# The second half of a closing RMS norm: factor from a square root and a reciprocal of two columns, sent over a diagonal

## What is computed

```python
def rmsnorm(x, g):
    y = x * lax.rsqrt(jnp.mean(x * x, axis=-1, keepdims=True) + 1e-6)
    return y * g

x = x + 0.5 * swiglu(rmsnorm(x, ffn2_norm), w_gate, w_up, w_down)
return rmsnorm(x, final_norm)
```

## Time and profile before

| | |
|---|---|
| median of 3 runs | 1667.12 us (1665.48 to 1675.3: 1675.3, 1667.12, 1665.48) |
| the profiled execution, its own time | 1676.78 us |
| span of the profiled execution | 1675.0 us |
| outside the span | 1.78 us |
| mean granted TensorE clock | 0.986 of full |

### The profile page before, as it was taken

One profiled execution on the slowest core, in us unless ns is written; L12 is line 12 of the kernel. 1 busy time (PEld: TensorE's weight loads), 2 busy tenths in 40 slices (PEclk: granted clock), 3 DMA queues, 4 the chain that ended last, 5 costly groups with the idle time before them and its releaser, 6 DMA issues.

```text
span 1675.0 us, 22081 instructions
## 1 busy us (share of the span) xinstructions
PE 1643.0 (98%) x8648; PEld 1327.8 (79%) x8648; DVE 813.1 (49%) x1342; ACT 686.1 (41%) x1232; POOL 267.2 (16%) x225
## 2 busy tenths in 40 slices
PE   9999999899999999999999999999999999999997
PEld 6777777777888888877888888877877888888887
DVE  5566435556655542255444433347465544443333
ACT  7565546545443343245333333344133533333222
POOL 1221110301322220002222210000020032223000
PEclk9997989999999999999999999999999999999999
DMA  5221000222333333313332233332222233222332
GB/s 197 77 89 39 15 26 14 95 81 88 101 101 101 101 92 94 97 58 113 101 101 92 97 92 103 87 119 83 70 87 83 95 101 101 92 97 86 104 97 79
DMA packets 45399, 148.50 MB, mean 89 GB/s; under 512 B 5193, under 2 KB 8433, under 8 KB 45297
## 3 DMA queue, kind: packets, MB, share of 16 engines
q1 hardware_dynamic: 41760, 142.10, 27.2%
q10 hardware_dynamic: 3536, 5.00, 0.9%
HBM read 144.98 MB, written 2.10 MB: 88 GB/s over the span
## 4 chain that ended last, share of the span: by engine, by line
PE 92%; DVE 3%; ACT 3%; issue 1%; DMA 1%; POOL 0%; DVEq 0%; SPq 0%; ACTq 0%; POOLq 0%
PE bank L257 90%; PE bank L378 1%; DMA raw<-in_w_in 1%; ACT hi L998 0%; DVE lo L1661 0%; PE bank L430 0%; ACT sq L1017 0%; PE bank L438 0%; DVE acc L1677 0%; DMA raw<-in_w_out 0%; ACT L1028 0%; DVE hs L2362 0%; DVE B L2284 0%; DVE x L2429 0%; DVE y L2219 0%
## 5 line engine op out<-in xcount | busy, mean ns | idle before, releaser
L1661 DVE TENSOR_TENSOR lo<-raw,hi 128x512 fp32r<-128x512 f32 (+1 forms) x514 | 392.2, 787 | 603.6 <-ACT hi L998 603.3
L257 PE MATMUL bank<-xh,hi 128*128 128x512 f32 x1576 | 613.2, 396 | 6.5 <-issue 2.0
L257 PE MATMUL bank<-xh,lo 128*128 128x512 f32 x1576 | 603.5, 390 | 1.2 <-DVE lo L1661 1.2
L257 PE MATMUL bank<-xl,hi 128*128 128x512 f32 x1576 | 596.3, 390 | 0.0
L998 ACT ACTIVATE hi<-raw 128x512 fp32r<-128x512 f32 (+1 forms) x540 | 321.6, 616 | 458.2 <-PE bank L257 413.9
L257 PEld LDWEIGHTS bank<-xh,hi 128*128 128x128 f32 x1576 | 296.2, 188 | 79.7 <-issue 10.9
L257 PEld LDWEIGHTS bank<-xh,lo 128*128 128x128 f32 x1576 | 296.6, 188 | 64.6 <-DVE lo L1661 2.1
L257 PEld LDWEIGHTS bank<-xl,hi 128*128 128x128 f32 x1576 | 296.6, 188 | 63.4 <-issue 3.1
L257 PE MATMUL bank<-fH,hi 128*128 128x512 f32 (+1 forms) x550 | 210.1, 382 | 0.0
L257 PE MATMUL bank<-fH,lo 128*128 128x512 f32 (+1 forms) x550 | 209.3, 381 | 0.0
L257 PE MATMUL bank<-fL,hi 128*128 128x512 f32 (+1 forms) x550 | 209.3, 381 | 0.0
(11 more groups left out here) (387 smaller groups left out, 1147.2 us busy)
## 6 DMA issues: line engine op xcount, KB each, us to landing
raw<-in_ffn_w_up SPq DMA_DIRECT2D x88, 512.0 KB, 3.4
raw<-in_w_in SPq DMA_DIRECT2D x50, 512.0 KB, 3.5
raw<-in_ffn_w_down SPq DMA_DIRECT2D x48, 512.0 KB, 3.5
raw<-in_ffn_w_gate SPq DMA_DIRECT2D x44, 512.0 KB, 3.5
raw<-in_ffn_w_down SPq DMA_DIRECT2D x24, 384.0 KB, 3.0
raw<-in_w_out SPq DMA_DIRECT2D x16, 512.0 KB, 3.4
x<-in_xt SPq DMA_DIRECT2D x8, 256.0 KB, 6.0
x<-in_xt ACTq DMA_DIRECT2D x8, 256.0 KB, 5.1
```

The lines of the kernel that those rows point to most:

```text
L257: return pe.matmul(out, w, x, start=start, stop=stop, skip_group_check=True)
L1661: dve.tensor_tensor(k.lo[i % CUT][:, 0:w], k.raw[u % RAW][:, at:at + w], k.hi[i % CUT][:, 0:w].bitcast(F), SUB).then_inc(k.cut_tail[i % 2], 1)
```

## The change

For the second half (h = 1) alone, the way from the squares to the factor is another one:

- TensorE, `row_sums`: now the blocks of `acc` and `sq[1]` are the weights and one column of ones the moving operand, two blocks of 128 tokens each. The result has tokens on partitions: 128x2. The `acc` part that stood after t = 12 is gone from the loop and stands after it, ahead of the wait for the square.
- ScalarE, `root`: square root of (sum/1024 + eps), 128x2, out of PSUM. `root_table` (a one-element Sqrt) takes the place of `log_table`.
- VectorE, `diagonal`: reciprocal of the 128x2, then the identity times it, a 128x256 tile in `acc2` with the factors on two diagonals.
- TensorE, `row_factor`: ones as weights by that tile, 256 columns: the factor of each token in every partition, in PSUM.
- VectorE, `write(1, n)`: reads the factor from PSUM instead of from `rB`.
- VectorE: `last_tile(1)` stands after all eight writes of the first half instead of after four, followed by `diagonal`.

A tile `rt` of 128x4 is allocated after `acc2`, so what is allocated behind it moves.

```diff
+COLS = [slice(0, 256), slice(256, 512)]
+HALVES = {7: -1}
@@ TensorE
+def row_sums(pe, k, i, h):
+    b, n = k.uses.take(("norm", i, h), 7)
+    room(pe, k, b, n)
+    pe.wait_ge(k.both, i + 1)
+    out, blocks = k.bank[b], [slice(256 * h + 128 * c, 256 * h + 128 * c + 128) for c in range(2)]
+    for c, at in enumerate(blocks):
+        mm(pe, out[:, c:c + 1], k.acc[:, at], k.ones[:, 0:1], c == 0, False)
+    pe.wait_ge(k.last_sq, k.last_sq_at[i] + h)
+    for c, at in enumerate(blocks):
+        m = mm(pe, out[:, c:c + 1], k.sq[1][:, at], k.ones[:, 0:1], False, True)
+    m.then_inc(k.full[b], 1)
+
+def row_factor(pe, k, i, h):
+    b, n = k.uses.take(("factor", i, h), 6 + h)
+    room(pe, k, b, n)
+    pe.wait_ge(k.diagonal, HALVES[i] + h + 1)
+    mm(pe, k.bank[b][:, COLS[h]], k.ones, k.acc2[:, COLS[h]], True, True).then_inc(k.full[b], 1)
@@ tensor_finale
-            if h == 1 and t == 12:
-                last_sums(pe, k, 1, cols[1])
-    end_last_sums(pe, k, 1, cols[1])
+    row_sums(pe, k, 7, 1)
+    row_factor(pe, k, 7, 1)
@@ ScalarE
+def root_table(act, k):
+    act.activation(k.eps[:, 2:3], k.eps[:, 0:1], ACT.Sqrt)
+
+def root(act, k, i, h):
+    b, _ = k.uses.at["norm", i, h]
+    act.wait_ge(*k.full_at(("norm", i, h)))
+    act.activation(k.rt[:, 2 * h:2 * h + 2], k.bank[b][:, 0:2], ACT.Sqrt, scale=1.0 / 1024,
+                   bias=k.eps[:, 0:1]).then_inc(k.read[b], 1)
@@ scalar_finale
     last_factor(0)
-    log_table(act, k)
+    root_table(act, k)
     last_square(1)
-    last_factor(1)
+    root(act, k, 7, 1)
@@ VectorE
+def diagonal(dve, k, i, h):
+    at, r = HALVES[i] + h + 1, k.rt[:, 2 * h:2 * h + 2]
+    dve.wait_ge(*k.read_at(("norm", i, h)))
+    dve.reciprocal(r, r).then_inc(k.inverted, 1)
+    dve.wait_ge(k.inverted, at)
+    dve.tensor_tensor(k.acc2[:, COLS[h]].rearrange("p (c t) -> p c t", c=2),
+                      k.ident.unsqueeze(1).broadcast_to([128, 2, 128]), r.unsqueeze(2).broadcast_to([128, 2, 128]),
+                      MUL).then_inc(k.diagonal, 1)
@@ vector_finale, write(h, n)
-        dve.wait_ge(k.rB_made, 8 + h)
+        if h == 0:
+            dve.wait_ge(k.rB_made, 8)
+        else:
+            dve.wait_ge(*k.full_at(("factor", 7, 1)))
+        factor = k.bank[k.uses.at["factor", 7, 1][0]] if h else k.rB
-        dve.scalar_tensor_tensor(..., scalar=k.col("final_norm_2", n), in1=k.rB[:, o],
+        dve.scalar_tensor_tensor(..., scalar=k.col("final_norm_2", n), in1=factor[:, o],
@@ vector_finale, loop over stores
-        if i == 4:
+        if i == 8:
             last_tile(1)
+            diagonal(dve, k, 7, 1)
@@ build
-        k.acc, k.acc2 = new("acc", T), new("acc2", T)
+        k.acc, k.acc2, k.rt = new("acc", T), new("acc2", T), new("rt", 4)
+        k.inverted, k.diagonal = sem("inverted"), sem("diagonal")
```

More of the change, by code:

```diff
@@ L2425, in write @@
         o = cols[h]
-        dve.wait_ge(k.rB_made, 8 + h)
+        if h == 0:
[3 more added lines that the diff above has]
+        factor = k.bank[k.uses.at["factor", 7, 1][0]] if h else k.rB
         if n == 7:
             dve.wait_ge(*k.read_at(("last", h)))
-        dve.scalar_tensor_tensor(out=k.xt[n][:, o], in0=k.xt[n][:, o], scalar=k.col("final_norm_2", n), in1=k.rB[:, o],
+        dve.scalar_tensor_tensor(out=k.xt[n][:, o], in0=k.xt[n][:, o], scalar=k.col("final_norm_2", n), in1=factor[:, o],
                                  op0=MUL, op1=MUL).then_inc(k.normed, 1)
```

## The result

The changed kernel's median is 1693.64 us (1693.28 to 1706.4, six runs) against 1666.97 us for the kernel before (1665.07 to 1678.79, six runs). The ratio, changed kernel to kernel before, is 1.0166, 95% interval 1.0135 to 1.0197. It is 27 us slower, where no measurable change was forecast, and far outside the range. The profiled execution took 1706.4 us, with a span of 1704.6 us against 1675.0; its mean granted clock was 0.984 against 0.986, so the two traces can be compared.

What follows compares the result with a forecast made beforehand. The prediction took the TensorE matmul stream (92% of the span) as the bound, with only the tail reachable: -0.72 us from square to first write and -0.04 from the add, -0.76 off 1667.12, giving 1666.4 us, range 1664.4 to 1674.6.

Steps and rivals of the forecast that it cites:

- The matmuls at either end alone: Whole kernel: a stream of matmuls, 92% TensorE; the change reaches only the last 9.37 us and some matmuls just before.
- Rival 3: All matmuls: tiles moved by rt change the pitch, 1% or 15 us slower, 1682; chance 0.03.
- The acc sum: End of the matmul stream: ends 0.43 us earlier, but the last add moves only -0.04, bounds -0.43 and +0.17.
- Narrow sums: Tail, TensorE after the square: four passes taking 0.52 us, ends 0.35 and 0.66, replacing 0.71.
- Root: Tail, ScalarE: 128x2 square root out of PSUM taking 0.25 us, ends 0.19 and 0.35; no table load on the path.
- Reciprocal and product: Tail, VectorE `diagonal`: the pair takes 0.62 us, ends 0.55 and 0.75.
- Factor: Tail, TensorE matmul pair over the ones: 0.71 us, ends 0.59 and 1.42 at half clock.
- Writes from PSUM: Second half's eight output writes: no change, 0, with ends -0.2 and +0.4 us over the eight.
- Rival 1: ScalarE tail: Square missing from the Sqrt table, two loads cost 2.56 us, +1.8 in all, 1668.9; chance 0.07.
- Rival 4: Second half's writes wait on something else and start at 1669.5 as before; chance 0.14 together with rival 2.
- rival 2: Tail: halved TensorE clock or slow order takes the gain, whole -0.05 us, 1667.0 to 1667.1; chance 0.14 with rival 4.
- The sum of the tail: From square's end to first write 2.29 us against 3.01, -0.72; with the add's -0.04, -0.76 us.

Runs made afterwards that it cites:

- the add after four writes: Changed kernel with rt allocated ahead of the pad, last_tile(1) back behind four first-half writes: span 1667.8 us, tail 13.77 us.
- rt ahead: Changed kernel with rt allocated ahead of the pad, so later tiles keep their old addresses: ratio 0.9992 against the kernel before, span 1662.7 us, tail 14.12 us.
- experiment 5: Tail comparison of changed kernel variants with rt allocated ahead of the pad: alone 14.12 us, add after four writes 13.77, add after seven plus extra matmuls 14.28.
- only xl odd: Kernel before with 32 unused bytes ahead of xl and 480 behind, so xl lies off by 32 bytes and the weights moved by 512: 1687.6 us.
- fours of a kind: Kernel before with products grouped in fours, once with lo off by 32 bytes (span 1696.1 us, 0.230 each), once with xl off (0.232 each).
- Fillers: Changed kernel, rt ahead of the pad, last tile's second add behind seven writes, six extra ones matmuls in the tail: ratio 1.0007, tail 14.28 us.

## Why the prediction was wrong

- **The matmuls at either end alone.** "No small change can move it but at its ends" was the step that failed. The change allocates a tile, and that moved the weights against the streamed tiles. The term was missing from the sum, so at nothing; it stood only as rival 3, with a chance of 0.03 and 15 us. It measured 27 us in the changed kernel, 26 with an unused tile alone. Rival 3 had 1% on all matmuls; what came is 3% on those of xh and xl and nothing on those of fH and fL.
- **The argument against rival 3** took the equal pitch with xh and with fH as proof that place is nothing. Both distances from the weights, 1024 and 0 modulo 2048, are multiples of 256 bytes. The rows compared two even distances, and no odd one, which the prediction did say ("no row shows this very shift") and then gave too small a chance. The pad in `build`, which aligns xh to 2048 bytes, was in the code to be read.
- **The acc sum** left the loop. The last tile's add still didn't come earlier, as worked out: 3.18 us behind the first write of half 0, where it was 3.20 (1695.53 - 1692.35, 1665.65 - 1662.45). The bound of -0.43 is what the add after four writes gives back (0.35 measured).
- **Narrow sums:** 0.62 us in the chain against 0.52 taken; within the ends. **Root:** 0.27 against 0.25. **Reciprocal and product:** 0.64 with the step between against 0.62. The step from the product to the factor's matmul was 0.14 us instead of 0.04.
- **Factor:** 0.68 us at full clock (rt ahead), 1.01 in the changed kernel, where the clock fell within it. I had taken one fall, 4.1 us after the end of the stream, as a limit that a pair starting 2.9 us after it would keep. The falls lie 3.3 to 5.3 us after the end of the stream in the traces of experiment 5, so that it held with rt ahead was luck.
- **Writes from PSUM:** eight took 3.22 us against 3.25. Right at 0.
- **Rival 1** fell: the square ran at 1695.98 behind the one-element Sqrt with no load before it. By the rule of the Trainium skill (ScalarE: Activation LUTs, Table sets) cheap functions are in every set; it doesn't name Square there, and for Square with Sqrt this trace agrees. **Rival 4** fell: the first write starts at 1699.19, 0.03 us behind the factor's pair.
- **Slips in the working.** Narrow sums, root and add at their slow ends give 0.45 us more, so -0.31 and not the -0.05 of a slow clock, as rival 2 has it. All stated ends together give -1.8 and +0.9 us, not -1.4 and +0.3. The range of the time didn't rest on either.
- **The sum of the tail** was -0.76 us; it came as -0.67 with `rt` ahead and -0.31 in the changed kernel. Of the 0.36 between them 0.33 are the factor pair at the lower clock, which no run ties to the addresses. The mechanism was right there, but it was 0.05% of the time, beside a term of 1.6%.

## What to carry to other kernels

A new tile in SBUF is an edit to every tile allocated behind it. In a kernel bound by matmuls like these, keep the distance between the tiles that stream and the weight tiles at a multiple of 256 bytes, put small new tiles ahead of a pad or at the end, and compare the pitch of untouched matmuls before and after, in stretches of equal granted clock: if it changed with the count unchanged, try the kernel before with nothing but an unused tile of the new size. Fillers in a relay must be shorter than the wait that they stand in; here they were not, and cost more than they kept.

## What the runs showed that was not expected

- fp32r matmuls of 128x512 with 128x128 weights go at 0.227 us each when streamed tile and weights lie a multiple of 256 bytes apart, and at 0.233 when they lie 32, 64 or 128 bytes off it: 3% on a stream that fills the engine. Alternating products take the slow pace for one odd tile in three (0.233; 0.231 in one stage with only xl odd), fours of a kind lie between (0.230 and 0.232), and a stretch of 24 takes its own. Why is not shown.
- The scatter of one kernel's runs goes with the mean granted clock. Of the changed kernel, runs with spans of 1691.5 to 1692.0 had 0.993, one of 1697.4 had 0.990, and the profiled one of 1704.6 had 0.984. In the kernel before, the clock of the profiled execution was 0.95 over the first 380 us and 1.00 over the next 360; with rt ahead 0.98 and 1.00. The difference between these executions is early, in the first 380 us.
